# Norm, projections and gates of a hybrid block in one stage

## What is computed

```python
h = rms_norm(x, ln_mix)
proj = h @ w_in          # qkv 1536, z 512, b 4, a 4, sb_q 512, sb_k 512, sb_v 512
q, k, v = split(silu(causal_conv4(qkv)))      # q, k are l2-normalised per head
beta = sigmoid(b)
g = -exp(a_log) * softplus(a + dt_bias)
gc = cumsum(g)                                # within a chunk
decay = exp(where(i >= j, gc[i] - gc[j], -inf))
lower = where(i > j, beta * (k @ k.T) * decay, 0)
qk = (q @ k.T) * decay
u, w = solve(lower + eye, [v * beta, k * beta * exp(gc)])
for each chunk:
    v_new = u - w @ state
    o = (q * exp(gc)) @ state + qk @ v_new
    state = state * exp(g_last) + (k * exp(g_last - gc)).T @ v_new
z = silu(z)                                   # gates o later
```

## Time and profile before

| what | value |
|---|---|
| median of 3 runs | 1987.03 us |
| lowest and highest run | 1983.39 and 1987.62 us |
| profiled execution, its own time | 1985.47 us |
| its span | 1983.7 us |
| mean granted TensorE clock | 0.901 |
| TensorE products busy | 1630.1 us, 82% |
| TensorE weight loads busy | 918.1 us, 46% |
| VectorE busy | 531.5 us, 27% |
| ScalarE busy | 390.1 us, 20% |
| GpSimd busy | 261.8 us, 13% |

### The profile page before, as it was taken

The page is one execution under the profiler, slowest core; times in us unless marked ns, Lnnn a source line. Parts: engine busy times, 40 slices in busy tenths (PEclk is TensorE's granted clock), DMA queues, the critical chain, the costliest instruction groups (busy, mean ns, idle before and its releaser), DMA issues. The chain is left out here.

```text
span 1983.7 us, 19944 instructions
## 1 busy us (share of the span) xinstructions
PE 1630.1 (82%) x7009; PEld 918.1 (46%) x7009; DVE 531.5 (27%) x671; ACT 390.1 (20%) x669; POOL 261.8 (13%) x386
## 2 busy tenths in 40 slices
PE   6999999995489899999938993777787778884997
PEld 3554444464367777777724553222222223332443
DVE  3223100003444444444422224111111111111332
ACT  2321100002133333343311210000000000003221
POOL 1000000000122222212211111111111111110110
PEclk9999999986699988999969995888888999896999
DMA  6212220100011111000062112599999999993120
GB/s 204 74 63 69 80 85 21 43 0 2 28 45 27 27 26 26 26 15 11 0 268 88 69 48 96 222 409 400 396 406 401 398 398 400 399 394 111 69 103 32
DMA packets 91072, 296.56 MB, mean 149 GB/s; under 512 B 14704, under 2 KB 48800, under 8 KB 65056
## 3 DMA queue, kind: packets, MB, share of 16 engines
q1 hardware_dynamic: 81536, 279.35, 36.9%
q0 software_dynamic: 9504, 16.80, 2.3%
HBM read 275.13 MB, written 38.80 MB: 158 GB/s over the span
## 5 line engine op out<-in xcount | busy, mean ns | idle before, releaser
L1421 PE MATMUL pe_gu<-w_gu,xT 128*64 128x512 f32 x1024 | 274.9, 698 | 105.9 <-DMA w_gu<-in_w_expert_up 102.4
L227 PE MATMUL pst<-hT,w_ct 128*128 128x512 f32 x640 | 278.6, 596 | 6.1 <-DMA w_ct<-in_w_in 6.1
L1421 PEld LDWEIGHTS pe_gu<-w_gu,xT 128*64 128x64 f32 x1024 | 84.3, 158 | 274.5 <-issue 272.8
L227 PEld LDWEIGHTS pst<-hT,w_ct 128*128 128x128 f32 x640 | 121.6, 191 | 156.1 <-issue 149.8
L765 DVE TENSOR_TENSOR_SCAN Pm<-rem,Pm 128x128 f32<-128x128 f32 (+3 forms) x96 | 103.1, 1074 | 182.3 <-ACT brk L706 182.3
L838 POOL TENSOR_TENSOR wt<-brk,Pm 128x128 f32<-128x128 f32 (+3 forms) x96 | 83.0, 864 | 341.3 <-DVE Pm L765 341.3
L1089 PE MATMUL p_x<-w_o,mT 128*128 128x512 f32 x256 | 120.9, 628 | 2.4 <-DVE mx L1044 1.3
L1439 PE MATMUL pe_y<-w_d,hTe 128*64 128x512 f32 x512 | 115.5, 592 | 1.1 <-DVE ys L1519 1.1
L1514 DVE TENSOR_TENSOR hs<-sg,pe_gu 128x256 f32<-128x256 f32 x32 | 13.5, 421 | 380.2 <-ACT sg L1485 380.2
L1742 PE MATMUL f_pg<-w_gu,f_xT 128*128 128x512 f32 x256 | 114.4, 601 | 1.1 <-ACT f_xT L1660 1.1
L587 PE MATMUL LB<-qk_st 64*128 64x128 f32 (+3 forms) x192 | 95.0, 577 | 21.3 <-DMA qk_st<-sqk_d 20.3
(11 more groups left out here) (269 smaller groups left out, 1924.3 us busy)
## 6 DMA issues: line engine op xcount, KB each, us to landing
w_gu<-in_w_expert_gate SPq DMA_DIRECT2D x64, 1024.0 KB, 13.5
w_gu<-in_w_expert_up SPq DMA_DIRECT2D x64, 1024.0 KB, 15.5
w_d<-in_w_expert_down SPq DMA_DIRECT2D x64, 1024.0 KB, 8.8
w_ct<-in_w_in SPq DMA_DIRECT2D x20, 512.0 KB, 4.4
y_sb<-y_d SPq DMA_DIRECT2D x8, 1024.0 KB, 5.6
qkv_d<-y_sb SPq DMA_DIRECT2D x12, 512.0 KB, 2.7
gst<-qkv_d SPq DMA_DIRECT2D x8, 768.0 KB, 5.5
x_all<-in_x SPq DMA_DIRECT2D x8, 512.0 KB, 6.7
```

Of the source, the lines that this page charges most:

```text
L227: last = pe.matmul(ps[s][:, cols], w_ct[:, s, k, :], hT[:, k, cols], start=k == 0, stop=k == KT - 1)
L1421: last = pe.matmul(p_gu[e * CAP:(e + 1) * CAP, :], xT[:, s, k, e * CAP:(e + 1) * CAP], wv[:, e, :, k, :], start=k == 0, stop=k == KT - 1)
```

## The change

Norm, projections and gates become one block, `stage_front`.

- SP issues the weights of channel tile 0 behind x tile 3. TensorE starts the first half of tile 0 after four token tiles of the norm, and its second half after all eight. The order then is: tiles 1 to 7, z, tiles 8 to 19, v.
- b and a join z: 520 columns per token tile, as two products of 260 columns. The separate products L263 are gone. ScalarE takes silu of the z columns and copies the 8 others.
- The scalar work of the gates stands between the z tiles and channel tile 8 on ScalarE and VectorE; the cumulative sums come after tile 9.
- The three factors are put into one tile of 96 columns, transposed by TensorE after tile 10, stored to DRAM (rows_d), and read back by SP for each chunk into all partitions (row_b, 768 KB a chunk, two buffers). The p_row products are gone. Chunk c is done beside channel tile 12 + c: exponentials on ScalarE, differences and decay products on VectorE, row_q on GpSimd.
- row_k and ke are gone. In the mixers TensorE multiplies the state by k itself, and VectorE applies exp(gc) times the k factor as a per-token coefficient (coef) when it makes R, in four instructions instead of one.
- z_sb, the x tiles and mx share memory; ba_sb and ssq_sb are no longer kept.

The core of the diff:

```diff
+                for t in range(NT):
+                    sp.dma_start(x_sb[:, t, :], x_tok[:, t, :]).then_inc(x_in[t], 16)
...
+                    if t == NT // 2 - 1:
+                        load_w(0)
+                load_w(1)
+                sp.dma_start(w_tok[:], w_v[:, :, C_Z:C_Z + NZ]).then_inc(wz_in, 16)
...
+                for ct in range(NCT):
+                    sp.wait_ge(ch_done, ct + 1)
+                    if ct + 2 < NCT:
+                        load_w(ct + 2)
+                    if ct == NQK:
+                        sp.wait_ge(tok_done, 2 * NT)
+                        sp.dma_start(w_tok[:, :, 0:SW], w_v[:, :, C_SV:C_SV + SW]).then_inc(wv_in, 16)
+                        sp.wait_ge(tok_read, 2 * NT)
+                        sp.dma_start(S["z_d"].rearrange("(t p) n -> p t n", p=P), z_sb).then_inc(z_stored, 16)
...
+                    if ct == NQK + 2:
+                        sp.wait_ge(rows_ok, 1)
+                        sp.dma_start(rows_d, rows_sb[:]).then_inc(rows_st, 16)
+                        sp.wait_ge(rows_st, 16)
+                        load_rows(0)
+                        load_rows(1)
+                    if NQKV <= ct < NQKV + NT - 2:
+                        c = ct - NQKV
+                        sp.wait_ge(mat_done, c + 1)
+                        sp.wait_ge(rq_done, c + 1)
+                        load_rows(c + 2)
```

```diff
+                    sp.dma_start(row_b[:, c % 2], rows_v[c].unsqueeze(0).to_broadcast([P, 3, GH * P])).then_inc(row_in[c % 2], 16)
```

TensorE's order:

```diff
+                for t in range(NT // 2):
+                    transposes(t)
+                project(0, 0)
+                for t in range(NT // 2, NT):
+                    transposes(t)
+                project(0, 1)
...
+                for ct in range(1, NQK):
+                    project(ct, 0)
+                    project(ct, 1)
+                    square_sums(ct - 1)
+                pe.wait_ge(wz_in, 16)
+                for t in range(NT):
+                    for half in range(2):
+                        token_rows(2 * t + half, t, half, half * ZH, ZH)
+                    if t == 0:
+                        square_sums(NQK - 1)
+                for ct in range(NQK, NCT):
+                    project(ct, 0)
+                    project(ct, 1)
+                    if ct == NQK + 1:
...
+                        pe.matmul(p_cum[:, 0, :], upto[:], g[:], start=True, stop=True)
+                        pe.matmul(p_cum[:, 1, :], ones[:], g[:], start=True, stop=True).then_inc(pe_cum, 1)
+                    if ct == NQK + 2:
...
+                        pe.transpose(p_rows, cols[:].rearrange("p n i -> p (n i)"), ident[:]).then_inc(rows_tr, 1)
+                pe.wait_ge(wv_in, 16)
+                for t in range(NT):
+                    token_rows(2 * NT + t, t, t % 2, 0, SW)
```

GpSimd and the mixers:

```diff
+                    pool.wait_ge(egr_done, c + 1)
+                    pool.wait_ge(row_in[s], 16 * (c // 2 + 1))
+                    pool.tensor_tensor(row_q[:, hs], egr[:, s], row_b[:, s, 1, :].rearrange("p (h i) -> p h i", h=GH), ALU.mult).then_inc(rq_done, 1)
...
                     elif piece == "ks":
-                        pe.wait_ge(qe_ok, i + 1)
                         for h in range(GH):
-                            last = pe.matmul(GA[:, h, :], ke[:, h, :], St[:, h, :], start=True, stop=True)
+                            last = pe.matmul(GA[:, h, :], hd(k, h), St[:, h, :], start=True, stop=True)
                         last.then_inc(ks_done, 1)
...
                     elif piece == "ods":
+                        pe.wait_ge(qe_ok, i + 1)
...
-                        dve.tensor_tensor(R[:], vb[:], GA[:], ALU.add).then_inc(R_ok, 1)
+                        for h in range(GH):
+                            last = dve.scalar_tensor_tensor(R[:, h, :], GA[:, h, :], coef[:, ds(i * GH + h, 1)], vb[:, h, :], ALU.mult, ALU.add)
+                        last.then_inc(R_ok, 1)
...
-                            pool.tensor_tensor(qe[:], gst[:, s, 0:GH], row_q[:, hs, :], ALU.mult)
-                            pool.tensor_tensor(ke[:], gst[:, s, GH:2 * GH], row_k[:, hs, :], ALU.mult).then_inc(qe_ok, 1)
+                            pool.tensor_tensor(qe[:], gst[:, s, 0:GH], row_q[:, hs, :], ALU.mult).then_inc(qe_ok, 1)
```

More of the change, by code:

```diff
@@ new lines, in stage_front @@
+        hp_in, upto_in, v_step, a_step, pe_cum, rows_tr, rows_ok, rows_st = (sem(n) for n in (
+            "hp_in", "upto_in", "v_step", "a_step", "pe_cum", "rows_tr", "rows_ok", "rows_st"))
+        row_in = [sem("row_in0"), sem("row_in1")]
+        egr_done, diff_step, diff_done, exp_done, dk_done, mat_done, rq_done = (sem(n) for n in (
+            "egr_done", "diff_step", "diff_done", "exp_done", "dk_done", "mat_done", "rq_done"))
+        column = lambda ct: ct * P if ct < NQKV else C_SQ + (ct - NQKV) * P
@@ L136, in _ @@
-            @block.tensor
[L137 to L143, removed]
-                    for k in range(KT):
-                        last = pe.transpose(pst[t % 2][:, k, :], xn[:, t % 2, k::KT], ident[:])
-                    last.then_inc(tr_done, 1)
@@ L391, in _ @@
+                conv_and_silu(NQK + 2)
+                conv_and_silu(NQK + 3)
+                for c in range(NSQK):
+                    ct = NQKV + c
+                    s = ct % 2
+                    act.wait_ge(ch_done, ct + 1)
+                    act.wait_ge(y_stored[s], 16 * (ct // 2))
+                    act.activation(y_sb[:, s], ps[s][:], ACT.Copy).then_inc(ch_copied, 1)
+                    act.wait_ge(row_in[c % 2], 16 * (c // 2 + 1))
                     if c >= 2:
-                        act.wait_ge(mat_done, c - 1)
@@ L405, in link @@
                     dve.wait_ge(v_step, step[0])
[L406 removed]
+                th = lambda x: x.rearrange("p (t h) -> p t h", h=GH)
+                dve.wait_ge(taps_ok, 1)
+                for ct in range(NQK):
+                    convolve(ct)
                 dve.wait_ge(hp_in, 32)
+                dve.wait_ge(tok_read, 2 * NT)
                 link(dve.tensor_tensor(arg[:], ba_sb[:, :, GH:2 * GH], hp[:, 1, :].unsqueeze(1).to_broadcast([P, NT, GH]), ALU.add))
@@ L462, in _ @@
+                    dve.tensor_tensor(decay_kk[:, hs], dec[:, s], row(2), ALU.mult).then_inc(mat_done, 1)
             @block.gpsimd
             def _(pool):
+                pool.memset(neghalf[:], -0.5).then_inc(nh_done, 1)
+                pool.wait_ge(nh_done, 1)
+                for t in range(NT):
+                    pool.wait_ge(ss_done, t + 1)
+                    pool.tensor_scalar(rsx[:, t:t + 1], ssx[:, t:t + 1], 1.0 / D, EPS, ALU.mult, ALU.add).then_inc(ms_done, 1)
+                    pool.wait_ge(ms_done, t + 1)
+                    pool.tensor_tensor(rsx[:, t:t + 1], rsx[:, t:t + 1], neghalf[:], ALU.pow).then_inc(rs_done, 1)
```

518 lines of the change are left out of this document (208 added, 310 removed).

## The result

The changed kernel takes **1862.64 us**, the median of four runs (1860.23 to 1864.38), against 1985.21 for the kernel before beside it. The ratio is 0.9385 (95% interval 0.9362 to 0.9408).

What follows compares the result with a forecast made beforehand. TensorE was taken to bound the projections until 429 us, with engines waiting for one another in the gates stage. Front -112.9 and mixers -12.6 give -125.5: 1985.5 to 1860.0 profiled, plus 1.6 makes 1862 median; range 1846 to 1884.

Steps and rivals of the forecast that it cites:

- Old path of 111.0 replaced by 1.5: Last token product to the mixers: only v's evacuation (0.60) and the step between stages (0.9) stay; 109.5 us removed.
- z at 260 columns, 56.4: z with gate columns as two 260-column pieces, 256 records: 56.4 against 54.9 us, +1.5, bounds 0 and +5.3.
- Covers: Channel tiles 8 to 19 (13.7 us each) and v (54.9) hide the gates; without cover each chunk costs up to 10 us.
- rival of slow loads: Row loads from DRAM above 36 us each would lose the whole gain, giving 1990 us or more; chance 0.03.
- gates not hidden: A joint on the in-order queues of ScalarE or SP is late, costing 12 us, giving 1874; chance 0.15.
- Start, -5.9: Tile 0 in two halves with early weights: first half starts at 16.8, second ends at 38.1; gain 5.9, bounds 2.1 to 5.9.
- XT, -5.8: Mixers: without ke the scan is not slowed, and TensorE's wait for XT is 1.07 us in all heads; 5.8 us less.
- R, +2.1: Mixers: R as four VectorE instructions takes 0.95 against 0.69 us, +0.26 a head, 2.1 in all; bounds 0 and 5.3.
- The clock, -8.9 as half of 17.8: Seven later mixer heads lose 17.8 us to half clock; shorter XT waits were taken to save half, ends 0 and -17.8.
- signs of being wrong: TensorE waits between 31 and 427 us, row loads landing in over 20 us, or a head taking more than 56 us.
- in all: Mixers: the clock still falls in all seven later heads, giving 1871 us; chance 0.2.
- in none: Mixers: the clock falls in none of the seven later heads, giving 1853 us; chance 0.2.

Runs made afterwards that it cites:

- chunks behind v: Against the changed kernel, the eight chunks of decay matrices are made after the evacuation of v, first two row loads still early: 1911.38 us.
- whole start: Against the changed kernel, all transposes come before both halves of tile 0, whose weights are issued behind all of x: 1861.15 us.
- ke back: Against the changed kernel, GpSimd again makes a product of ke's old size behind qe in every head, result unused: 1874.7 us.
- gate columns apart: Against the changed kernel, z is in products of 512 columns and b, a in separate 8-column products behind z: 1888.24 us.
- XT first: Against the changed kernel, VectorE fills XT, then X, before the 256-column scan in each head: 1845.04 us, and 1846.56 once more.
- R by head: Against the changed kernel, TensorE starts each product when its quarter of R is there: 1848.04 us; together with XT first, 1837.94 us.
- mixers alone: Against the kernel before, only the mixers' edits: no ke, TensorE takes k, R by four instructions with coef, no row_k: 1973.06 us.

## Why the prediction was right

1862 was forecast and 1862.64 measured. The mechanisms held but for the start's, and the sizes of the start and of R were off the most. That the times agree to a microsecond is luck. For a profiled run the forecast was 1860.0 and the run took 1864.4; the medians agree better because the working added 1.6 for a profiled run below the median, and this one lay 1.7 above. And the same code gave a start that varied by 3 us between the profiles, a part behind the mixers that varied by up to 8, and mixers with three to six falls, worth 9 us.

- **Old path of 111.0 replaced by 1.5.** Right, but for the step between stages. It was read as 0.9 from the earlier trace rows; from the end of the last evacuation (427.61) to the first instruction (429.03) it was 1.4.
- **z at 260 columns, 56.4.** Measured 56.6. The line through two sizes served for a third one. Scaling by columns alone would have given 55.8 (54.9 x 520/512), so the lower bound of this term should have been +0.9 and not 0; and the old z was 128 records of 512 columns, not the "256 as before".
- **Covers.** All held, first with no wait of TensorE between 33 and 427 us. The row loads landed in 6.7 us, near the 7.6 of gst that they were held against; the rival of slow loads, and that of gates not hidden, are out. The run with the chunks behind v shows the worth of the chunks' cover, 46 us.
- **Start, -5.9.** It was -3.8 in this profile, inside its bounds of 2.1 to 5.9; the eight other profiles with the same start have -3.9 to -0.8, four of them outside. Two parts of the step failed: the first half started at 17.38 and not 16.8, and it took 8.34 (to the next transposes, at 25.72) and not 6.9. So the choice that transposes ahead of either half would keep the clock up was wrong: here one spell of low clock was paid, in the first half, and the second half took its 6.9; in three other profiles both halves paid. The run with the whole start, which has no such spell, shows further that the split itself, to which the step gave the gain, did nothing.
- **XT, -5.8.** 14.3 to 8.7 is -5.6, and the scan is at 751 ns in all sixteen. The run with ke back shows that it is this product. The Trainium skill, "SBUF — State Buffer", section "SBUF: two separate sides", has the loser of the shared port pair wait to the end of the other's instruction. With ke back the scan began 0.84 before ke ended and lost 1.39 - 0.75 = 0.64, as in the trace before: the direction agrees, the size is three quarters. The 1.3 us that the prediction would add by that rule would not have belonged to the term, which is a difference of measured waits.
- **R, +2.1.** It was +4.2 (6.9 to 11.1), inside the bounds; this is the worst-sized term. The group of four takes 1.13 and not 0.95: one of 128 columns is 345 ns, and the next starts 0.26 us later ((1.13 - 0.345) / 3), of which the columns are 0.13 (an estimate: 1.22 us for 1024 columns in the earlier trace rows and 0.69 for 512 in the earlier trace rows make 0.13 for 128). The wait grew by more than the group did (0.53 against 0.44 a head).
- **The clock, -8.9 as half of 17.8.** Four falls remained of seven. Three falls fewer at about 2.9 is -8.7. The price of 2.5 a fall that the working implies was a little low, and the half, a guess between two ends, came near the count: luck, since the same mixers fell in three heads with the gate columns apart and in six with the whole start. The first head, on which the guess leaned, was a poor witness: it stayed up in all nine kernels in which its wait was 1.06 to 1.29 us, while later heads fell behind waits of 0.97 to 1.14.

Against the forecast for a profiled run: start 2.1, R 2.1, step 0.5, XT 0.2 and clock 0.2 make 5.1 too low, the run 4.4. The 0.7 left lies in the front (111.0 measured, 112.9 forecast, with 2.6 named), 0.3 of it in the shorter step from VectorE's first instruction to the first product; the rest was not traced.

Two of the prediction's own signs of being wrong did show, both small. TensorE waits 1.32 us before the second half of tile 0, at 31.7 to 33.0, since the start ran late; and heads 3 and 7 took 56.5 and 56.9 us, over the 56 named, for the 56 left no room for a table load and a fall in one head. Two sums of it don't close: its own terms give 1842 and 1881 for the ends of the range (1853 - 2.1 - 9, and 1874 + 3.2 + 3.8), where it has 1846 and 1884; and 550.72 less 112.9 puts the first product of the mixers at 437.8, where it has 439. Neither touches the forecast.

The rivals on the clock were real ones. Over all profiled runs, with a first XT wait of 1.7 to 2.2 us (before and ke back) 14 of 14 later heads fell; with one of 0.97 to 1.14 (seven kernels) 26 of 49; with one of at most 0.3 (XT first, twice, and with R by head) 0 of 21. So the case "in all" was near (start whole has six of seven), and the case "in none" was one reordering away. What decides between falling and not at a wait of 1.1 stays open. Three kernels with quite different fronts (after, mixers alone, chunks after v) fall in the same four heads, which hardly looks like chance from head to head; but the same instructions of the mixers fall in 2, 4 and 7 with the gate columns apart and in 2, 4, 5, 6, 7 and 8 with the whole start, so the mixers' code alone does not decide it either. Nor was a wait of the same length tried between large products.

## What to carry to other kernels

Ask of a stage that leaves TensorE idle whether its inputs exist before a long TensorE-bound stretch ends; beside such a stretch its work is free, if each joint of the in-order queues has room and the rows it needs can come by DMA. Very small products (8 columns) belong as extra columns in larger ones. A wait of about a microsecond between small products is dearer than it looks, for the clock may fall behind it (here 2.9 us each time, in 26 heads of 49): look there first for a reordering on the engine that TensorE waits for, and hand results over in the pieces in which they are used.

## What the runs showed of the hardware

- One GpSimd product of 1.26 us beside a VectorE scan lengthened the scan by 0.64 us (1.39 against 0.75), and with the clock cost the mixers 13.7 us over eight heads. Also a VectorE product of 128x512 with both inputs in SBUF took 0.97 to 1.58 us in the run with the chunks behind v, where GpSimd's product overlapped it, and 0.69 where it did not:

```profile
431.71 1.27 POOL L439 TENSOR_TENSOR row_q<-sq_sb,row_b 128x512 f32<-128x512 f32 x1 [412.01 <-ACT sq_sb L327]
...
432.19 1.34 DVE L420 TENSOR_TENSOR sq_sb<-sq_sb,r_k 128x512 f32<-128x512 f32 x1 [161.05 <-ACT sq_sb L329]
...
444.25 0.69 DVE L420 TENSOR_TENSOR sq_sb<-sq_sb,r_k 128x512 f32<-128x512 f32 x1 [0.70 <-ACT sq_sb L329]
```

- Products of 8 columns took TensorE's clock to half while it was busy without a pause (28.00 of 28.00 us from 208 to 236, at 0.51), and the full-size products behind them paid for some 6 us more.
- A stretch of 6.8 us at half clock cost 2.5 to 3.0 us and not 3.4. The later XT waits are 15.7 us with seven falls (ke back), 16.5 with six, 17.3 with four and 18.7 with none: part of the lost time comes back as shorter waits.
